# A two-block layer on one core: tile 1's GLA output split around tile 0's first head, the first experts chosen from an 8 by 8 grid, the gather buffers in another order

## What is computed

```python
q = (xt @ w_q).reshape(T, PEER_HEADS, 2, PEER_HALF)             # 8 heads, 2 x 128
s = jnp.einsum('thpe,pne->thpn', q, sub_keys)                   # 128 scores a side
top_s, top_i = lax.top_k(s, 16)
cand = top_s[:, :, 0, :, None] + top_s[:, :, 1, None, :]        # 16 x 16 pairs
best_s, best_j = lax.top_k(cand.reshape(T, 8, 256), 16)
idx_a = jnp.take_along_axis(top_i[:, :, 0], best_j // 16, axis=-1)
idx_b = jnp.take_along_axis(top_i[:, :, 1], best_j % 16, axis=-1)
expert = idx_a * 128 + idx_b                                    # 16 experts a head and token
gate = jax.nn.softmax(best_s, axis=-1)
h = jnp.einsum('td,thkd->thk', xb, u[eb])
a = jax.nn.gelu(h, approximate=False) * gb
out = jnp.einsum('thk,thkd->td', a, v[eb])
```

## Time and profile before

| | |
|---|---|
| median of 3 runs | 2069.77 us (2068.98 to 2069.86) |
| the profiled execution | 2069.34 us, its span 2067.5 us |
| granted TensorE clock, mean | 0.993 |
| PE busy | 1894.2 us (92%), 8012 records |
| DVE, ACT, POOL busy | 1382.8, 897.0, 618.5 us |
| DMA | 710.15 MB, mean 343 GB/s |
| gathers (POOL queue) | 550.15 MB |
| weight loads and the like (SP queue) | 158.34 MB |

### The profile page before, as it was taken

The page is one execution under the profiler, slowest core; times in us unless marked ns, Lnnn a source line. Parts: engine busy times, 40 slices in busy tenths (PEclk is TensorE's granted clock), DMA queues, the critical chain, the costliest instruction groups (busy, mean ns, idle before and its releaser), DMA issues. The chain is left out here.

```text
span 2067.5 us, 24834 instructions
## 1 busy us (share of the span) xinstructions
PE 1894.2 (92%) x8012; PEld 1168.6 (57%) x8012; DVE 1382.8 (67%) x2957; ACT 897.0 (43%) x2417; POOL 618.5 (30%) x563
## 2 busy tenths in 40 slices
PE   8999999999998999988989998999999899777776
PEld 7888678887955654432556644556565456222222
DVE  7788566666738767775765645766865566985444
ACT  5657454454634433333334623333455334343332
POOL 0002200000004444344433334343334434444442
PEclk9999999999999999999999999999999999999999
DMA  6633555544649999999999999999999999999996
GB/s 239 224 133 113 204 194 188 194 168 166 221 153 375 422 420 421 421 421 422 410 421 421 421 422 413 421 411 422 420 417 405 421 421 408 423 421 421 421 420 279
DMA packets 99373, 710.15 MB, mean 343 GB/s; under 512 B 11040, under 2 KB 11184, under 8 KB 14384
## 3 DMA queue, kind: packets, MB, share of 16 engines
q0 software_dynamic: 76928, 550.15, 64.5%
q1 hardware_dynamic: 22176, 158.34, 20.1%
q10 hardware_dynamic: 144, 0.11, 0.0%
HBM read 707.51 MB, written 1.05 MB: 343 GB/s over the span
## 5 line engine op out<-in xcount | busy, mean ns | idle before, releaser
L1454 PE MATMUL bank<-arena 128*128 128x512 f32 x2048 | 980.3, 609 | 149.2 <-ACT arena L2087 147.5
L2533 DVE SCALAR_TENSOR_TENSOR arena<-arena,x_tok 128x1024 f32<-128x1024 f32 x512 | 627.2, 1227 | 466.9 <-DMA arena<-peer_uv,arena 461.3
L2243 POOL DMA_INDIRECT arena<-peer_uv,arena x512 | 585.5, 1144 | 867.7 <-PE bank L1454 619.8
L1454 PEld LDWEIGHTS bank<-arena 128*128 128x128 f32 x2048 | 361.8, 191 | 642.0 <-ACT arena L2087 347.4
L2080 ACT ACTIVATE arena<-arena 128x1 f32<-128x1 f32 x512 | 103.5, 202 | 836.1 <-DVE arena L2533 835.3
L923 PEld LDWEIGHTS bank<-xT,weight_ring 128*128 128x128 f32 x1376 | 183.2, 193 | 41.5 <-issue 34.9
L2087 ACT ACTIVATE arena<-arena 128x128 f32<-128x128 f32 x512 | 197.7, 386 | 0.5
L2074 ACT ACTIVATE arena<-const_tile,arena 128x128 f32<-128x128 f32 x512 | 197.8, 386 | 0.0
L923 PE MATMUL bank<-xT,weight_ring 128*128 128x128 f32 (+1 forms) x1376 | 195.5, 294 | 0.8 <-DVE xT L2270 0.8
L923 PE MATMUL bank<-x_low_high,z_high 128*128 128x512 f32 (+1 forms) x480 | 135.9, 351 | 0.0
L1199 PE MATMUL bank<-x_split,w_split 128*128 128x512 f32 x704 | 127.4, 339 | 3.2 <-DVE x_split L2813 3.2
(11 more groups left out here) (321 smaller groups left out, 1990.5 us busy)
## 6 DMA issues: line engine op xcount, KB each, us to landing
weight_ring<-weights SPq DMA_DIRECT2D x149, 1024.0 KB, 5.0
arena<-peer_uv,arena POOLq DMA_INDIRECT x512, 15.0
row_ring<-rows_in POOLq DMA_DIRECT2D x8, 512.0 KB, 4.9
arena<-weights POOLq DMA_DIRECT2D x5, 512.0 KB, 7.4
kept_queries<-weights POOLq DMA_DIRECT2D x4, 512.0 KB, 9.8
const_tile<-consts POOLq DMA_DIRECT2D x1, 1657.0 KB, 8.5
x_tok<-x_in SPq DMA_DIRECT2D x2, 512.0 KB, 4.8
memT<-memT_in POOLq DMA_DIRECT2D x1, 1024.0 KB, 7.5
```

What stands on the lines that cost most here:

```text
L1454: ins = pe.matmul(b[:, :], diag[n % DIAGS], gbuf[n % GBUF][:, 1, h * 512:(h + 1) * 512], start=n % P == 0, stop=n % P == P - 1)
L2243: pool.indirect_dma_start(gbuf[n % GBUF].rearrange("p a d -> p (a d)"), None, peer_uv, bass.IndirectOffsetOnAxis(ap=expert[t][:, s:s + 1]. ...
L2533: dve.scalar_tensor_tensor(u, u, 1.0, x[:, t, :], ALU.mult, ALU.mult, accum_out=hdot[:, s:s + 1])\
```

## The change

Four edits.

1. PE's order. GLA output for tile 1 and head pair 0 runs in one piece before the transposes of tile 0's `x`, with the first chunk of head pair 1. The second chunk of head pair 1 comes one head at a time, around `head_tile_keys(0, 0)`. The three products of tile 1 with row chunks 6 and 7 that stood ahead of the GLA output now come behind it, with their `give_back`. `turn_mix(1)` comes behind these, after the keys. ACT's drains and squares, and `job_plan`, follow that order.
2. DVE's order. `first_expert` and `next_experts` come before `mixed_tile(1)`, and `other_experts` after it.
3. `next_experts` takes ranks 1 to 7 from the 8 by 8 grid of the best eight of each side, with 3-bit positions and one-hot rows of 8. A copy of the grid with the eight best taken out is kept, and `other_experts` puts it into the 16 by 16 grid, in place of a replace over 256.
4. The gather buffers lie at places 0, 1, 2, 3, 5, 6, 7, 4. Gather 0 also waits for the last of tile 1's GLA output, gather 5 for `mix_ready` 2 (place 6), and gather 7 instead of gather 4 for tile 1's output product (place 4).

```diff
 GBUF = 8
-MIX_BUF = 4
+GATHER_PLACES = (0, 1, 2, 3, 5, 6, 7, 4)
 DIAGS = 5
...
     plan("out0_0", 2, "dve", [2, 3])
+    plan("gla_o", 1, "dve", [0], first=2)
     plan("xT_peer0_0", 1, "act", [6])
-    plan("gla_o", 1, "dve", [0], first=2)
     plan("xT_peer0_0", 1, "act", [7], first=1)
+    plan("peer_q0_0_0", 1, "act", [2])
+    plan("peer_s0_0_0", 1, "act", [7])
     plan("gla_o", 1, "dve", [1], first=3)
-    plan("peer_q0_0_0", 1, "act", [2])
     plan("gla_mixT_1", 2, "act", [3, 6])
-    plan("peer_s0_0_0", 1, "act", [7])
...
-        gbuf = [area(2 * D * b, 2, D) for b in range(GBUF)]
         lo = 2 * D * GBUF
+        gbuf = [area(2 * D * b, 2, D) for b in GATHER_PLACES]
         sc = [area(lo + 2048 * t, 16, PN) for t in range(NT)]
         pq = [area(lo + 4096 + 512 * b, 2, S) for b in range(2)]
         rest = area(lo + 5120, 2 * TH * PN)
+        first_grid = area(lo + 5120 + 2 * PN, PK * PK // 4)
         onehot = area(lo + 5120, TH, PK, PK)
         top_v, top_i, top_f = (area(lo + 5632 + 64 * n, 2 * TH, PK) for n in range(3))
         best_v, best_j, pos_a, pos_b, sel_a, sel_b, pos_u = (area(lo + 5824 + 32 * n, TH, PK) for n in range(7))
...
-                def gla_out(t, hp, pars):
+                def gla_out(t, hp, pars, heads=range(2)):
...
                         o = slice(par * CH, (par + 1) * CH)
-                        for i in range(2):
+                        for i in heads:
...
                     out_rows(0, k, [h])
-            out_rows(1, NK - 2, [1])
-            out_rows(1, NK - 1)
-            give_back()
-            gla_out(1, 0, [0])
+            gla_out(1, 0, range(2))
+            gla_out(1, 1, [0])
             pe.wait_ge(sem("x_half_ready"), 1)
             turn_peer_half(0, 0)
-            gla_out(1, 0, [1])
             pe.wait_ge(sem("x_ready"), 5)
             turn_peer_half(0, 1)
-            gla_out(1, 1, range(2))
             wait_drained(pe, ("xT_peer0_0", 1))
             pe.wait_ge(sem("head_loaded"), 64)
             head_tile(0, 0, 0)
             head_tile(0, 1, 0)
+            gla_out(1, 1, [1], [0])
+            head_tile_keys(0, 0)
+            gla_out(1, 1, [1], [1])
+            out_rows(1, NK - 2, [1])
+            out_rows(1, NK - 1)
+            give_back()
             turn_mix(1)
-            head_tile_keys(0, 0)
             wait_drained(pe, ("gla_mixT_1", 1))
             for k in range(NK - 2):
...
             norm_root(0, 0)
+            gla_squares(2)
             turned_peer_half(0, 0)
-            gla_squares(2)
             turned_peer_half(0, 1)
+            head_tile(0, 0)
+            head_tile_keys(0, 0)
             gla_squares(3)
-            head_tile(0, 0)
             mix_turned(1)
-            head_tile_keys(0, 0)
             gate_exp(0, 0, 0, 1)
...
                 if n == 0:
+                    wait_filled(pool, ("gla_o", 3))
...
                     pool.wait_ge(sem("peer_experts"), ROUTE_NO[l, t, s])
-                if n == MIX_BUF:
+                if n == GATHER_PLACES.index(6):
+                    pool.wait_ge(sem("mix_ready"), 2)
+                if n == GATHER_PLACES.index(4):
                     wait_filled(pool, ("out0_1", 1))
                 if n >= GBUF:
...
-            def ranks_to_experts(l, t, h, first, last, name):
-
-                n = last - first
-                oh = onehot[:, 0, 0:n]
+            def ranks_to_experts(first, last, bits, name):
+
+                n, side = last - first, 1 << bits
+                oh = onehot[:, 0, 0:n, 0:side]
                 for q, (pos, sel) in enumerate(((pos_a, sel_a), (pos_b, sel_b))):
-                    op, val = (ALU.logical_shift_right, 4) if q == 0 else (ALU.bitwise_and, 15)
+                    op, val = (ALU.logical_shift_right, bits) if q == 0 else (ALU.bitwise_and, side - 1)
                     pos, sel, at = pos[:, 0, 0:n], sel[:, 0, 0:n], pos_u[:, 0, 0:n].bitcast(U32)
                     step(dve.tensor_scalar(at, best_j[:, 0, first:last].bitcast(U32), val, None, op))
                     step(dve.tensor_copy(pos, at))
-                    step(dve.tensor_tensor(oh, c("iota").unsqueeze(1).to_broadcast([P, n, PK]),
-                                           pos.unsqueeze(2).to_broadcast([P, n, PK]), ALU.is_equal))
-                    step(dve.tensor_tensor(oh, oh, top_f[:, q, :].unsqueeze(1).to_broadcast([P, n, PK]), ALU.mult))
+                    step(dve.tensor_tensor(oh, c("iota")[:, 0:side].unsqueeze(1).to_broadcast([P, n, side]),
+                                           pos.unsqueeze(2).to_broadcast([P, n, side]), ALU.is_equal))
+                    step(dve.tensor_tensor(oh, oh, top_f[:, q, 0:side].unsqueeze(1).to_broadcast([P, n, side]), ALU.mult))
                     step(dve.tensor_reduce(sel, oh, AX, ALU.add))
                 high, low = sel_a[:, 0, 0:n], sel_b[:, 0, 0:n]
-                step(dve.tensor_scalar(high, high, float(PN), float(l * EXPERTS), ALU.mult, ALU.add))
-                step(dve.tensor_tensor(expert[t][:, h * PK + first:h * PK + last].bitcast(U32), high, low, ALU.add), name)
-
-            def first_head():
-
-                half, lowest = PK // 2, -3.0e38
+                step(dve.tensor_scalar(high, high, float(PN), 0.0, ALU.mult, ALU.add))
+                step(dve.tensor_tensor(expert[0][:, first:last].bitcast(U32), high, low, ALU.add), name)
+
+            def first_expert():
+
+                half = PK // 2
                 wait_drained(dve, ("peer_s0_0_0", 0))
                 keys = sc[0][:, 0:2, :]
-                left = rest[:, 0:2 * PN].rearrange("p (a n) -> p a n", a=2)
                 for q in range(2):
                     done(dve.max(top_v[:, q, 0:half], keys[:, q, :]), "dve_step")
                 settle()
...
                      "first_expert")
+
+            def next_experts():
+
+                half, lowest = PK // 2, -3.0e38
+                grid = rest[:, 0:half * half]
+                step(dve.tensor_tensor(grid.rearrange("p (a b) -> p a b", a=half),
+                                       top_v[:, 0, 0:half].unsqueeze(2).to_broadcast([P, half, half]),
+                                       top_v[:, 1, 0:half].unsqueeze(1).to_broadcast([P, half, half]), ALU.add))
+                best, at = best_v[:, 0, 0:half], best_j[:, 0, 0:half].bitcast(U32)
+                step(dve.max(best, grid))
+                step(dve.max_index(at, best, grid))
+                step(dve.match_replace(first_grid, best, grid, lowest))
+                ranks_to_experts(1, half, 3, "next_experts")
+
+            def other_experts():
+
+                half, lowest = PK // 2, -3.0e38
+                keys = sc[0][:, 0:2, :]
+                left = rest[:, 0:2 * PN].rearrange("p (a n) -> p a n", a=2)
                 for q in range(2):
                     done(dve.match_replace(left[:, q, :], top_v[:, q, 0:half], keys[:, q, :], lowest), "dve_step")
                 settle()
...
                 flat = keys.rearrange("p a n -> p (a n)")
-                step(dve.tensor_tensor(flat.rearrange("p (a b) -> p a b", a=PK),
-                                       top_v[:, 0, :].unsqueeze(2).to_broadcast([P, PK, PK]),
+                grid = flat.rearrange("p (a b) -> p a b", a=PK)
+                step(dve.tensor_tensor(grid, top_v[:, 0, :].unsqueeze(2).to_broadcast([P, PK, PK]),
                                        top_v[:, 1, :].unsqueeze(1).to_broadcast([P, PK, PK]), ALU.add))
+                step(dve.tensor_copy(grid[:, 0:half, 0:half], first_grid.rearrange("p (a b) -> p a b", a=half)))
                 best, at = best_v[:, 0, :], best_j[:, 0, :].bitcast(U32)
-                step(dve.max(best[:, 0:half], flat))
-                step(dve.max_index(at[:, 0:half], best[:, 0:half], flat))
-                ranks_to_experts(0, 0, 0, 1, half, "next_experts")
-                others = rest[:, 0:2 * PN]
-                step(dve.match_replace(others, best[:, 0:half], flat, lowest))
-                step(dve.max(best[:, half:PK], others))
-                step(dve.max_index(at[:, half:PK], best[:, half:PK], others))
+                step(dve.max(best[:, half:PK], flat))
+                step(dve.max_index(at[:, half:PK], best[:, half:PK], flat))
                 step(dve.tensor_tensor(gate_w[0][:, 0, :], best, best[:, 0:1].to_broadcast([P, PK]), ALU.subtract),
                      "peer_shifted")
-                ranks_to_experts(0, 0, 0, half, PK, "peer_experts")
+                ranks_to_experts(half, PK, 4, "peer_experts")
                 normalised_gates(0, 0, 0, 1)
 
             def sides_onehot(q, size):
...
             first_norm()
+            first_expert()
+            next_experts()
             mixed_tile(1)
-            first_head()
+            other_experts()
             for n in range(SLOTS + 2 * LATER + 1):
                 for name, what in DVE_STEPS.get(n, []):
                     if name == "second_sum":
```

## The result

| | before | the change |
|---|---|---|
| median | 2070.44 us (20 runs, 2066.52 to 2073.92) | 2073.07 us (20 runs, 2070.44 to 2076.87) |
| ratio | | 1.0013, 95% interval 1.0007 to 1.0019 |
| profiled execution, its span | 2069.34 us, 2067.5 | 2076.82 us, 2075.0 |
| granted TensorE clock, mean | 0.993 | 0.991 |

The change makes the kernel 2.6 us slower. That is less than the 0.2% named in the prediction, but clear of zero, and 0.3 us outside the range.

The account below looks back on a forecast made before the run. The prediction took the DMA stream from about 626 us as the bound: -0.4 us at its start plus +0.4 for PE's delay made 0.0, so 2069.8 us, range 2067.4 to 2072.8.

Follow-up runs that it names:

- e4: The kernel before with 24 products of the identity (5.6 us) added on PE ahead of tile 1's last twelve products; ratio 1.0010 to the kernel before.
- e7: The changed kernel with head 2's query, keys and routing two slots later; ratio 1.0011 to the kernel before.
- e8: The changed kernel with mixed_tile(1) ahead of next_experts and one tile 1 product moved into PE's 0.8 us stop before the first head query; ratio 0.9994 to the kernel before.
- e2: The changed kernel with 18 products of the identity with itself filling PE's stop ahead of turn_mix(1); ratio 1.0006 to the kernel before.

## What to carry to other kernels

When a stream is the bound, look for the shallowest point of its cover, and measure what depth it needs from a stretch that really ran dry, not from the first one with its share taken off. An early start of the stream and a delay of the engine that gives its buffers back draw on the same cover: a gain of 0.3 us was bought with a delay of 5.5. And a signal that another engine is out of work for (`mix_ready` 2) should go out before work whose result can queue (ranks 1 to 7): this exchange alone turned 1.0013 into 0.9991.

## What the runs showed of the hardware

The low clock behind a stop can outlast it. In the earlier trace rows a stop near 636 us had 3.4 us of it; the 4.25 us stop was followed by 6.8 us (0.83 over 20 us), and 12.9 us instead of 10.4 for twelve products. A stop's length alone does not settle it here: every kernel has the same 2.86 us stop ahead of slot 0, and over 640 to 660 the clock was 1.00 in the change, e4, e7 and e8, and 0.83 to 0.96 in the kernel before and the others. Filling the stop with idle products, whose results nobody reads, kept the clock at its upper level: 1.00 over 620 to 640 in e2, and 2.5 us back at the end of its trace.
